# RWKV-7 recurrence in four 64x64 tiles of TensorE, identity products in place of adds, and fewer passes ahead of the first projection

## What is computed

```python
def step(state, inp):
    r_t, w_t, k_t, v_t, kk_t, a_t = inp
    sk = jnp.einsum('bhij,bhj->bhi', state, kk_t)
    state = (state * w_t[:, :, None, :]
             - sk[..., None] * (kk_t * a_t)[:, :, None, :]
             + v_t[..., None] * k_t[:, :, None, :])
    y = jnp.einsum('bhij,bhj->bhi', state, r_t)
    return state, y
...
mean = jnp.mean(y, axis=-1, keepdims=True)
var = jnp.mean(jnp.square(y - mean), axis=-1, keepdims=True)
y = ((y - mean) * lax.rsqrt(var + GN_EPS)).reshape(b, s, d) * ln_w + ln_b
```

## Time and profile before

| | |
|---|---|
| median of three runs | 2944.93 us |
| profiled execution | 2938.78 us |
| its span | 2937.0 us |
| TensorE, matmul records busy | 2683.2 us (91%) |
| VectorE / ScalarE / GpSimd busy | 1589.4 / 948.4 / 1246.0 us |
| HBM read | 297.77 MB |
| run-in of the recurrence | 1641 to 1716 us |
| full periods | 1716 to 2033 us |
| last periods | 2033 to 2107 us |

### The profile page before, as it was taken

How to read it: one execution, slowest core, us unless ns; L and a number is a source line. 1 busy time by engine, 2 the same in 40 slices (tenths; PEclk the granted TensorE clock), 3 DMA queues, 4 the chain that set the end, 5 groups by cost and what they waited for, 6 DMA issues and landing times. The chain is left out here.

```text
span 2937.0 us, 51498 instructions
## 1 busy us (share of the span) xinstructions
PE 2683.2 (91%) x21600; PEld 2204.9 (75%) x21600; DVE 1589.4 (54%) x2030; ACT 948.4 (32%) x1615; POOL 1246.0 (42%) x630
## 2 busy tenths in 40 slices
PE   1878888999999999989999599999799999999999
PEld 1565667788887788767777488888787888788887
DVE  5754454665553633366865478888435333333334
ACT  2434433322214222244544233343334222222221
POOL 2532224544435444444344335444356444444443
PEclk9989999999999999999999899999999999999999
DMA  6421224345442222237566444444232222223223
GB/s 242 154 93 37 86 83 154 128 174 172 165 136 86 94 100 101 94 102 187 156 172 158 115 97 98 95 95 87 89 122 86 101 97 97 87 93 108 94 100 122
DMA packets 299013, 341.94 MB, mean 116 GB/s; under 512 B 214560, under 2 KB 214688, under 8 KB 298784
## 3 DMA queue, kind: packets, MB, share of 16 engines
q1 hardware_dynamic: 298784, 338.65, 37.3%
HBM read 297.77 MB, written 39.85 MB: 115 GB/s over the span
## 5 line engine op out<-in xcount | busy, mean ns | idle before, releaser
L709 POOL TENSOR_TENSOR wl<-w,wh 128x1024 fp32r<-128x1024 f32 x367 | 902.3, 2465 | 1278.6 <-ACT wh L750 1278.3
L180 PE MATMUL ps<-hi,wh 128*128 128x512 f32 x2208 | 884.6, 401 | 21.7 <-ACT qk_raw L787 10.0
L181 PE MATMUL ps<-lo,wh 128*128 128x512 f32 x2208 | 869.8, 394 | 0.0
L182 PE MATMUL ps<-hi,wl 128*128 128x512 f32 x2208 | 869.3, 394 | 0.0
L750 ACT ACTIVATE wh<-w 128x1024 fp32r<-128x1024 f32 x367 | 386.9, 1056 | 684.3 <-DMA w<-in_ffn_w_in 523.0
L1021 DVE SCALAR_TENSOR_TENSOR xt<-ps,mod,xt 128x512 f32<-128x512 f32 x384 | 286.4, 749 | 425.2 <-PE ps L182 417.8
L180 PEld LDWEIGHTS ps<-hi,wh 128*128 128x128 f32 x2208 | 420.9, 191 | 124.9 <-issue 33.6
L181 PEld LDWEIGHTS ps<-lo,wh 128*128 128x128 f32 x2208 | 421.4, 191 | 90.3 <-issue 3.7
L182 PEld LDWEIGHTS ps<-hi,wl 128*128 128x128 f32 x2208 | 420.2, 190 | 90.2
L1026 DVE TENSOR_TENSOR act<-ps,silu 128x512 f32<-128x512 f32 x88 | 60.8, 691 | 482.2 <-PE ps L182 482.2
L180 PE MATMUL ps<-act_hi,wh 128*128 128x512 f32 x704 | 282.3, 401 | 16.4 <-DVE act_lo L1030 9.7
(11 more groups left out here) (225 smaller groups left out, 3443.2 us busy)
## 6 DMA issues: line engine op xcount, KB each, us to landing
w<-in_ffn_w_in SPq DMA_DIRECT2D x176, 512.0 KB, 3.3
piece<-in_ada_w SPq DMA_DIRECT2D x96, 512.0 KB, 5.0
w<-in_ffn_w_out SPq DMA_DIRECT2D x88, 512.0 KB, 3.3
w<-in_w_rkv SPq DMA_DIRECT2D x48, 512.0 KB, 3.8
scratch<-silu SPq DMA_DIRECT2D x48, 256.0 KB, 3.0
scratch<-act SPq DMA_DIRECT2D x48, 256.0 KB, 2.8
w<-in_wqk SPq DMA_DIRECT2D x20, 512.0 KB, 4.7
xt<-in_xT SPq DMA_DIRECT2D x4, 2048.0 KB, 11.8
```

The costliest lines, as they stand in the source:

```text
L180: pe.matmul(out, w_hi(k), x_hi(k), start=first and k == 0, stop=False)
L181: pe.matmul(out, w_hi(k), x_lo(k), start=False, stop=False)
L182: ins = pe.matmul(out, w_lo(k), x_hi(k), start=False, stop=last and k == kc - 1)
L709: pool.tensor_tensor(wl[n % NW][:, :, :], wr[n % NW][:, :, :], wh[n % NW][:, :, :].bitcast(F32), ALU.subtract).then_inc(*wlo.up)
```

## The change

Nine things are changed; the first seven lie in the recurrence.

1. The heads of pairs 4 to 7 write to the other half of the partitions in `by_token`, `gram`, `level_x`, the first product of `level_t`, `solve_u` and the products of keys and values, so that all four 64x64 tiles are addressed in turn. Products of a tile and the state, the second product of a level and `by_feature` stay on the two tiles of the diagonal. Results lie in two PSUM banks (`spot`, `two_banks`).
2. `level_x` adds the identity as a product of the identity with itself in PSUM; ScalarE copies 1+X out whole. VectorE's `level` is gone.
3. ScalarE takes out each result of a level in one instruction.
4. `solve_x` is split: `known_x`, which needs no state, stands first, then `by_feature`, then the product with the state.
5. `outputs` and `state_products` are one step, the product with the state last; VectorE steps the state first and then centres, ahead of the masks.
6. The mean is scaled inside its subtraction.
7. The transposed diagonal blocks come back in four DMAs for a chunk, not two.
8. The rotary angles: one range reduction; the cosine is the sine of pi/2 less the absolute value.
9. The four weight tiles no longer stand ahead of piece 15: three of them and the second half of x follow it.

```diff
@@ level_x, level_t
-                            for q in range(2):
-                                if l == 0:
-                                    pe.wait_ge(*g["w_done"].at(NQ * ch))
-                                else:
-                                    pe.wait_ge(*g["t_done"].at(NQ * ch + 2 * l - 2 + q + 1))
-                                for j, hs in heads(0, QP):
-                                    jj = q * QP + j
-                                    ins = pe.matmul(quarter(q)[hs, j, :], ntm[l][ch % len(ntm[l])][hs, jj, :], (tdiag[ch % 2], tinv, tdiag[ch % 2])[l][hs, jj, :],
-                                                    start=True, stop=True)
-                                ins.then_inc(*g["x_done_w"].up)
+                            for j, to, hs in heads():
+                                pe.matmul(spot(0, j, to), idst[hs], idst[hs], start=j % QP == 0, stop=False)
+                            for j, to, hs in heads():
+                                ins = pe.matmul(spot(0, j, to), ntm[l][ch % len(ntm[l])][hs, j, :], (tdiag[ch % 2], tinv, tdiag[ch % 2])[l][hs, j, :],
+                                                start=False, stop=j % QP == QP - 1)
+                            ins.then_inc(*g["x_done_w"].up)
...
+                            if l < NL - 1:
+                                for j, hs, to in heads():
+                                    ins = pe.matmul(spot(0, j, to), old[hs, j, :], wx[l % 2][hs, j, :], start=True, stop=True)
                                 ins.then_inc(*g["tr_done"].up)
+                            for j, hs, _ in heads():
+                                ins = pe.matmul(bank(2)[hs, j, :], wx[l % 2][hs, j, :], old[hs, j, :], start=True, stop=True)
+                            ins.then_inc(*g["tr_done"].up)
@@ the order of the heads
+                def away(j, h):
+
+                    return home(j, h if j < QP else 1 - h)
+
+                def heads(pairs=PAIRS):
+
+                    for i in range(pairs // 2):
+                        for j in (i, i + pairs // 2):
+                            for h in range(2):
+                                yield j, home(j, h), away(j, h)
@@ solve_x
+                        def solve_x(ch):
+                            pe.wait_ge(*g["s_done"].at(ch))
+                            pe.wait_ge(*g["x_known"].at(ch + 1))
+                            for j, hs, _ in heads():
+                                ins = pe.matmul(spot(3, j, hs), ar[ch % (RING + 1)][hs, j, 0, :], state[hs, j, :], start=False, stop=j % QP == QP - 1)
                             ins.then_inc(*g["xs_done"].up)
@@ ScalarE, level
+                        def level(ch, l):
+                            act.wait_ge(*g["x_done_w"].at(NL * ch + l + 1))
+                            act.activation(in_two(wx[l % 2]), two_banks(0), ACT.Copy).then_inc(*g["w_done"].up)
                             if l < NL - 1:
...
@@ VectorE
-                        def level(ch, l, q):
-                            pairs = slice(q * QP, (q + 1) * QP)
-                            dve.wait_ge(*g["x_done_w"].at(NQ * ch + 2 * l + q + 1))
-                            dve.tensor_tensor(wx[l % 2][:, pairs, :], quarter(q), idst.unsqueeze(1).to_broadcast([P, QP, CHUNK]),
-                                              ALU.add).then_inc(*g["w_done"].up)
...
+                            dve.scalar_tensor_tensor(in_two(yc), mean[:, :].rearrange("p (b a) -> p b a", b=2).unsqueeze(3).to_broadcast([P, 2, QP, CHUNK]),
+                                                     -1.0 / HEAD, two_banks(3, HALF // 2), ALU.mult, ALU.add).then_inc(*g["yc_done"].up)
@@ the angles
-                            for j, quarter in enumerate((0.0, 0.25)):
-                                after(dve.tensor_scalar(turns, ang, 1.0 / TWO_PI, quarter, ALU.mult, ALU.add))
-                                after(dve.tensor_scalar(turns, turns, ROUND, None, ALU.add))
-                                after(dve.tensor_scalar(turns, turns, ROUND, None, ALU.subtract))
-                                if j == 1:
-                                    dve.wait_ge(*trig_done.at(1))
...
+                            after(dve.tensor_scalar(turns, ang, 1.0 / TWO_PI, ROUND, ALU.mult, ALU.add))
+                            after(dve.tensor_scalar(turns, turns, ROUND, None, ALU.subtract))
...
+                            dve.scalar_tensor_tensor(turns, red, -1.0, red, ALU.mult, ALU.max).then_inc(*red_done.up)
```

More of the change, by code:

```diff
@@ L634, in _ @@
                         for step, *e in plan.order:
-                            if step == "part" and e[1] == 0:
+                            if step == "part" and e[1] == 0 and tiles[e[0]][0] == "ada" and tiles[e[0]][-1] == 1:
+                                pass
+                            elif step == "part" and e[1] == 0:
                                 load(top[e[0]] + AHEAD + 1)
@@ L1624, in by_token @@
                                 pe.wait_ge(*g["b_out"].at(ch + 1))
-                            for j, hs in heads(0, PAIRS):
-                                ins = pe.matmul(bank(6)[hs, j, :], (vt_[ch % 2], bdec, kdec)[n][hs, j, :], idst[hs], start=True, stop=True)
+                            for j, hs, to in heads():
+                                ins = pe.matmul(spot(3, j, to), (vt_[ch % 2], bdec, kdec)[n][hs, j, :], idst[hs], start=True, stop=True)
                             ins.then_inc(*g[("v_tok", "b_tok", "k_tok")[n]].up)
@@ L1691, in state_products @@
-                        def state_products(ch):
-                            b = ch % RING
-                            for j, hs in heads(0, PAIRS):
-                                pe.matmul(bank(6)[hs, j, :], ktok[b][hs, j, :], vtok[ch % (RING + 1)][hs, j, :], start=True, stop=False)
-                                ins = pe.matmul(bank(6)[hs, j, :], btok[b][hs, j, :], ust[hs, j, :], start=False, stop=True)
+                            pe.wait_ge(*g["yc_done"].at(ch))
+                            for j, to, hs in heads():
+                                pe.matmul(spot(3, j, to, HALF // 2), gk[b][hs, j, 1, :], vtok[ch % (RING + 1)][hs, j, :], start=j % QP == 0, stop=False)
@@ new lines, in outputs_and_state @@
+                            for j, to, hs in heads():
+                                pe.matmul(spot(3, j, to), ktok[b][hs, j, :], vtok[ch % (RING + 1)][hs, j, :], start=False, stop=False)
+                            for j, to, hs in heads():
+                                pe.matmul(spot(3, j, to, HALF // 2), arb[b][hs, j, :], ust[hs, j, :], start=False, stop=False)
+                            for j, to, hs in heads():
+                                ins = pe.matmul(spot(3, j, to), btok[b][hs, j, :], ust[hs, j, :], start=False, stop=False)
@@ new lines, in outputs_and_state @@
+                            ins.then_inc(*g["y_known"].up)
+                            for j, hs, _ in heads():
+                                if j < QP:
+                                    pe.matmul(spot(3, j, hs, HALF // 2), ar[ch % (RING + 1)][hs, j, 1, :], state[hs, j, :], start=False, stop=j % QP == QP - 1)
+                            pe.wait_ge(*g["y_known"].at(ch + 1))
+                            for j, hs, _ in heads():
+                                if j >= QP:
+                                    ins = pe.matmul(spot(3, j, hs, HALF // 2), ar[ch % (RING + 1)][hs, j, 1, :], state[hs, j, :], start=False, stop=j % QP == QP - 1)
@@ L1903, in period @@
                                 affine(zp)
-                            if y is not None:
-                                level(y, 0, 0), level(y, 0, 1)
                             if d is not None:
@@ L1923, in period @@
                                 variance(zz)
-                            if y is not None:
-                                level(y, 2, 0), level(y, 2, 1)
                             if x is not None:
```

160 lines of the change are left out of this document (73 added, 87 removed).

## The result

The changed kernel takes 2962.25 us (median of four runs, 2959.28 to 2968.52) against 2940.55 us of the kernel before (four runs): ratio 1.0073, 95% interval 1.0047 to 1.0099. The forecast was 2906 us, range 2884 to 2935. The profiled execution has a span of 2958.9 us, 21.9 more than before.

What follows compares the result with a forecast made beforehand. The prediction took TensorE's queue to bound the recurrence, and VectorE's angles, then DMA, the start. From 2938.8 us profiled, 14 for the start and 18 for the recurrence came off, giving 2906.8, stated as 2906, range 2884 to 2935.

Steps and rivals of the forecast that it cites:

- (b): Recurrence loop: by_feature now stands ahead of solve_x, so x_st starts at +4.6 us after the root, losing 0.8 us.
- (c): Recurrence loop: ScalarE's roots, values, exponentials and p_end take 4.0 us, then the copy of 1+X 0.5, ending at +9.1.
- (d): Recurrence loop: level 0, solve_u and u_st end at +11.9 us; clock falls, priced separately, add 1.7 in half the periods.
- (e): Recurrence loop: four groups of 0.47 us, the state product 0.93 and 0.2 more, ending at +15.0.
- (f): Recurrence loop: VectorE's state, decay, reduce and centre, with half of GpSimd's slowing, take 3.3 us, ending at +18.3.
- (g): Recurrence loop: VectorE's five masks of 0.62 us and k_dec of 0.6, ending at +21.9.
- (h): Recurrence loop: gram, level 2, last inverse and roots close the period at 24.95 us, 1.4 less than before.
- rival A: Recurrence: four tiles don't keep 0.47 us with 64 columns; 0.86 a group, period 27.3, kernel 2935 us; chance 0.17.
- Rival D: Recurrence: TensorE at 1.2 GHz for most of each period makes the kernel slower, 2954 us and more; chance 0.05.
- The last three intervals: End of the recurrence: 6 us saved of 50.5, bounds 0 and 14.
- The run-in: Ahead of the recurrence's full stretch (1641 to 1716): 5 us saved, bounds 0 and 12.
- The start: Angles and first loads: first projection matmul 16 to 19 us earlier, 14 us of it kept, bounds 5 and 19.

Runs made afterwards that it cites:

- e1: Changed kernel with each level's identity added by two wide products in place of 32 of 64x64: 2936.15 us, ratio 1.0016.
- e8: Changed kernel with the 8x8 blocks' way back through DRAM issued ahead of the chunk's loads and the blocks' way out: 2950.38 us, ratio 1.0038.
- e9: e7 with the sync engine's edit of e8: 2904.06 us, ratio 0.9883.
- e6: Changed kernel with the identity added by VectorE again and ScalarE no longer copying 1+X: 2937.91 us, ratio 1.0004.
- e12: e9 with the identity as 32 products of 64x64 again: 2929.37 us, ratio 0.9971.
- e7: e5 with ScalarE squaring the next keys ahead of the roots and level 1's first product behind the outputs: 2932.95 us, ratio 0.9986.
- e5: e1 with by_feature behind solve_x instead of ahead of it: 2938.98 us, ratio 1.0011.
- e2: Changed kernel with all heads kept in the two tiles of the diagonal: 2994.55 us, ratio 1.0214.
- e10: e9 with all heads in the two tiles of the diagonal: 2982.31 us, ratio 1.0143.
- e3: Kernel before with only the changed angles and order of the first loads: 2922.24 us, ratio 0.9967.
- e4: Changed kernel with 24 repeats of a 64x64 group in four tiles and as many products in two: 768 records took 21.7 and 22.6 us.

## Why the prediction was wrong

The steps of the loop, in us after the root's end, as means over the twelve full periods of each trace (e9 has its own order):

| | forecast | changed | e1 | e8 | e9 |
|---|---|---|---|---|---|
| (b) x_st starts | 4.6 | 4.84 | 4.82 | 4.89 | 2.65 |
| (c) copy of 1+X ends | 9.1 | 9.57 | 9.60 | 9.31 | 7.19 |
| (d) u_st ends | 11.9 | 13.24 | 12.95 | 12.23 | 9.99 |
| (e) last product with the state ends | 15.0 | 18.80 | 17.32 | 18.07 | 13.89 |
| (f) centred | 18.3 | 21.80 | 20.31 | 21.11 | 17.01 |
| (g) k_dec ends | 21.9 | 25.40 | 23.90 | 24.70 | 20.79 |
| (h) root, the period | 24.95 | 28.70 | 27.21 | 27.90 | 24.90 |
| clock low (1.2 GHz) in the twelve, us | 20 | 37 | 17 | 20 | 0 |

- **The pace of four tiles was right**: 0.67 to 0.69 us in the rows, so rival A did not come true. That TensorE stops being the bound, and that the period becomes a loop through the engines, was right too. (b), (c), (f), (g) and (h), each taken from the step before, hold within 0.4 us.
- **Step (e) failed**: 3.1 us forecast, 5.6 measured. It took each group at 0.47 us back to back. From solve_u to the last product with the state stand eight groups, 512 instructions, two loads: 4.2 us of work at the pace (the last at 0.93), and up to 7.5 us at that of the loads. The stands inside the output groups and those with the state (L1709 to L1723) are 19 us in the twelve periods, 1.6 us in each. I had a group's pace from bursts of 32 records, shorter than a load, and carried it to eight groups in a row. (e) also left out that level 1's two products stand between u_st and the outputs: after u_st's end at 1901.95 the outputs begin at 1902.47, 0.5 us. Of e1's gain of 1.5 us in a period 1.2 lie in this step. e6 gains 0.9 in it and 2.3 ahead of it, and loses 1.8 in (h). e12 loses against e9 in (b), (d), (f) and (h), and hardly in this one: the loads take their toll wherever a new one is due.
- **Step (d) took 0.9 us more**, by the clock. In six periods it takes 2.8 us, as forecast; in the six others the clock is low for 2.4 to 4.8 us of it and it takes 4.2 to 5.0 (in the longest TensorE also waits for diag_t). So the low clock costs about 1.6 us there, near the 1.7 that I had, and in half of the periods, as I had taken it. The forecast has this in a term of its own.
- **Step (f)** has a small error of its own: I put half of GpSimd's slowing on it, 0.5 us. The state times its decay takes 0.69 us in eight of the twelve periods, and 0.97 to 1.67 in the four in which GpSimd runs beside it, 0.2 us a period. The figure of 25.3 us for the whole loss is a slip: by the same rows it is 25.5.
- **"They are issued in the period before their use" was wrong** of the diagonal's DMAs. They and diag land just ahead of their use, as the sync engine issues them behind a wait for VectorE's masks. In a faster loop that costs 1.0% (e7 against e9); in the changed kernel 0.35% by the ratios of e8, which isn't clear of the difference between chips. I had looked at where the step stands in the code, not at when its rows stand relative to TensorE's.
- **A loss where nothing waits for the gain.** (b) was named as a loss of 0.8 us and priced right, but e5 shows that undoing it alone gives nothing: a loop has to be shortened at the step that ends last.
- **The clock** was low for 37 us of the twelve periods, where I had 20. Rival D (low for nine of 25 us in each period) is not what happened: 37 of 344. The traces with falls in the twelve periods (changed, e1, e5 to e8, e12) have single stands of 2.1 us and more; the longest is 1.0 us in e2, 1.9 in e9 and 0.7 in e10, and there the clock stays at 1.00. Six of the eight falls of the changed kernel begin 8.0 to 11.8 us after the root, at the stand of (c) or just behind it, the other two at +18.4 and +19.0. No run changes the clock alone, so what part of the 28.4 us is its own beyond (d) stays open.
- **The last three intervals** grew by 9 where I had −6; the same groups follow each other there with fewer others between, but no run takes this stretch by itself, so its cause isn't shown. e9 has 52.2 us for them, 1.7 more than before.
- **The run-in** gained 7.6 us against 5, at a mean clock of 0.74.
- **The start** gave 10.9 of the 14 us (e3: it keeps them). The missing part is one row. Changed kernel, VectorE and GpSimd at the first norm:

```profile
50.67 1.28 DVE L1145 SCALAR_TENSOR_TENSOR ada_acc<-piece,cact,ada_acc 128x1024 f32<-128x1024 f32 x1 [0.90 <-DMA piece<-in_ada_w]
...
53.45 7.41 POOL L711 TENSOR_TENSOR wl<-w,wh 128x1024 fp32r<-128x1024 f32 x3 [17.06 <-ACT wh L752]
...
55.99 5.42 DVE L1164 SCALAR_TENSOR_TENSOR t<-xt,gain,squares 128x512 f32<-128x512 f32 x2 [0.20 <-DVE mod L1041]
...
62.22 0.77 PE L181 MATMUL ps<-hi,wh 128*128 128x512 f32 x1 [6.63 <-DVE lo L1168]
```

Before the change, the same two instructions:

```profile
70.66 1.41 DVE L1164 SCALAR_TENSOR_TENSOR t<-xt,gain,squares 128x512 f32<-128x512 f32 x2 [0.20 <-DVE mod L1038]
```

The last piece begins 14.6 us earlier than in the earlier trace rows. But the weights now land behind it, so GpSimd splits three of them just when VectorE applies the first norm: two instructions of L1164 take 5.42 us where the same two took 1.41 before, 4.0 us lost. That GpSimd's splits slow them is read from the overlap alone; no run moves the one and not the other. I had written that what is moved must still be moved, and priced only its transfer.

Summed on the profiled execution: forecast −32.0, measured +21.9. Periods 2.9 us each beyond the forecast with its falls (24.95 + 0.85): 35; last intervals 15; start 3; behind the last root 3; run-in −2.6. Together 53.4 of 53.9.

## What to carry to other kernels

A small matmul cost two things here: its work in its tile, and the bytes of its instructions. Before small products are made twice as dense, count the instructions in the longest dense stretch and compare with the pace at which the loads of instructions came in the trace; fewer, wider products can win although they do more work. When a bound engine is relieved, every path that used to be early has to be timed again, transfers through DRAM and the queue that issues them first: its rows, not its place in the code, say how early it is.

## What the runs showed that I had not expected

- Instructions come in loads of 256, and 256 of TensorE's take 3.75 us to follow each other when it waits for them (e4): 14.6 ns each. Two-tile 64x64 records in fp32 use them up in just this time.
- Records in four different tiles start 14.6 ns apart on average for 128 in a row, a weight load with each.
- In the waits, a stand for instructions shows as "issue". So do a wait for a copy out of the same PSUM banks (L1647) and e7's wait for diag (L1661, up to 3.5 us). What tells them apart is the place, inside a group, where no semaphore is, and the end of the stand, 1.2 to 1.7 us after a load of q8 has landed.
- e7's twelve runs span 36 us, e5's and e6's ten 19 and 21, while e12, whose clock falls too, spans 12 in ten and the kernel before 15 in twenty. What makes e7 vary so, no run says.
